# Two square sums of a hybrid decoder step in column groups, and its key pages dealt out differently

## What is computed

```python
h = x
for i in range(2):
    hn = rms_norm(h, g_pre[i])
    if i == 0: out, s = gla_mixer(hn, ...)       # q, k, v, g projections, recurrence, output projection
    else:      out = sb_mixer(hn, ...)           # q1, g1 projections, attention over K, V, output projection
    h = h + out
    h = h + sigmoid(rms_norm(h, g_ple[i]) @ w_ple_gate[i]) * (p[i] @ w_ple_up[i])
    if i == 0: k_new, v_new = split(rms_norm(h, g_kv) @ w_kv)
return rms_norm(h, g_final), states, k_new, v_new

def rms_norm(x, g):                              # over the 1024 features of a token
    return x * rsqrt(mean(x * x, axis=-1) + 1e-6) * g
```

## Time and profile before

| | |
|---|---|
| median of 3 runs | 893.49 us (893.46 to 893.99) |
| the profiled execution | 891.69 us, span of its trace 890.0 us |
| mean granted TensorE clock | 0.991 |
| busy: PE, DVE, ACT, POOL | 846.0, 553.3, 456.5, 277.9 us |
| HBM traffic | 231.6 MB, 260 GB/s |

### The profile page before, as it was taken

The page is one execution under the profiler, slowest core; times in us unless marked ns, Lnnn a source line. Parts: engine busy times, 40 slices in busy tenths (PEclk is TensorE's granted clock), DMA queues, the critical chain, the costliest instruction groups (busy, mean ns, idle before and its releaser), DMA issues.

```text
span 890.0 us, 14818 instructions
## 1 busy us (share of the span) xinstructions
PE 846.0 (95%) x5057; PEld 586.4 (66%) x5057; DVE 553.3 (62%) x678; ACT 456.5 (51%) x1529; POOL 277.9 (31%) x149
## 2 busy tenths in 40 slices
PE   5999999999999999999998999999989999999995
PEld 3666667767754444454487878778744444799995
DVE  4555475679856869989995632232267777555553
ACT  5611382236658677759772422212288766444433
POOL 3000000865776998994970000000100000021110
PEclk9999999999999999999999999999999999999997
DMA  9799868656599998988995069998898879221202
GB/s 332 273 372 399 314 228 286 215 156 216 187 311 368 377 329 306 333 330 312 344 385 189 1 234 327 357 342 305 306 331 296 320 272 362 101 95 49 95 1 96
DMA packets 109531, 232.52 MB, mean 261 GB/s; under 512 B 7473, under 2 KB 66680, under 8 KB 109456
## 3 DMA queue, kind: packets, MB, share of 16 engines
q1 hardware_dynamic: 50992, 172.16, 53.1%
q10 hardware_dynamic: 58464, 59.41, 20.0%
HBM read 220.41 MB, written 11.14 MB: 260 GB/s over the span
## 4 chain that ended last, share of the span: by engine, by line
PE 71%; DVE 8%; DMA 7%; ACT 6%; issue 4%; POOL 2%; SPq 1%; ACTq 0%; POOLq 0%; DVEq 0%
PE pp L1659 18%; PE pp L1646 15%; PE pp L1662 9%; PE pp L2080 6%; PE pp L2037 4%; DMA s<-in_state_gla_dram 3%; POOL slot L621 2%; PE pp L2064 2%; DMA slot<-in_cache_k_dram 2%; PE pp L1623 2%; PE pp L1643 2%; PE pp L2051 2%; PE pp L1674 2%; DMA slot<-in_cache_v_dram 1%; ACT slot L827 1%
## 5 line engine op out<-in xcount | busy, mean ns | idle before, releaser
L621 POOL TENSOR_TENSOR slot<-slot,qb 128x1024 f32<-128x1024 f32 x95 | 246.9, 2629 | 101.8 <-DMA slot<-in_cache_k_dram 62.9
L1307 DVE TENSOR_REDUCE zall<-slot 128x16 f32<-128x1024 f32 x99 | 119.1, 1215 | 21.7 <-POOL slot L621 20.6
L1122 DVE TENSOR_TENSOR w_lo<-w_raw,w_hi 128x1024 fp32r<-128x1024 f32 x57 | 80.0, 1405 | 68.0 <-ACT w_hi L671 67.8
L827 ACT ACTIVATE slot<-slot 128x64 f32<-128x64 f32 x464 | 111.0, 241 | 20.5 <-POOL slot L621 20.5
L671 ACT CAST w_hi<-w_raw 128x1024 fp32r<-128x1024 f32 x58 | 60.5, 1045 | 79.0 <-PE pp L1662 47.1
L827 ACT ACTIVATION_READ_ACCUMULATOR slot<-slot 128x1 f32 x464 | 87.1, 188 | 0.0
L1646 PE MATMUL pp<-xn,w_raw 128*128 128x512 f32 x192 | 84.3, 593 | 0.5 <-ACT xn L682 0.5
L1646 PE MATMUL pp<-xn,w_unsplit 128*128 128x512 f32 x192 | 83.9, 592 | 0.0
L1662 PE MATMUL pp<-xa_hi,w_hi 128*128 128x512 f32 x200 | 81.5, 407 | 1.9 <-DVE w_lo L1122 1.9
L1659 PE MATMUL pp<-xb_hi,w_hi 128*128 128x260 f32 x384 | 78.9, 287 | 1.1 <-DVE w_lo L1122 0.9
L1662 PE MATMUL pp<-xa_hi,w_lo 128*128 128x512 f32 x200 | 79.2, 396 | 0.0
(11 more groups left out here) (321 smaller groups left out, 1435.8 us busy)
## 6 DMA issues: line engine op xcount, KB each, us to landing
slot<-in_cache_k_dram SPq DMA_DIRECT2D x128, 512.0 KB, 5.9
slot<-in_cache_v_dram SPq DMA_DIRECT2D x120, 512.0 KB, 5.8
w_raw<-in_gla_w_in_dram ACTq DMA_DIRECT2D x12, 1024.0 KB, 8.7
slot<-in_gla_w_in_dram SPq DMA_DIRECT2D x24, 512.0 KB, 9.4
w_raw<-in_w_kv_dram ACTq DMA_DIRECT2D x8, 1024.0 KB, 10.9
w_raw<-in_w_ple_gate_dram ACTq DMA_DIRECT2D x6, 1024.0 KB, 5.3
s<-in_state_gla_dram SPq DMA_DIRECT2D x1, 4096.0 KB, 27.3
out_dram<-s ACTq DMA_DIRECT2D x4, 1024.0 KB, 10.1
```

What stands on the lines that cost most here:

```text
L621: nc.gpsimd.tensor_tensor(slot[s][:], slot[s][:], qb[:, (n // NPG) % 2, :], ALU.mult).then_inc(S("k_mul_pool"), 1)
L827: ins = nc.scalar.activation(part, part, ACT.Copy, accum_out=zall[:, n % NPG, b * SH + h:b * SH + h + 1])
L1122: nc.vector.tensor_tensor(lo, raw, hi.bitcast(F32), ALU.subtract).then_inc(S("w_split"), 1)
L1307: nc.vector.tensor_reduce(zall[:, n % NPG, b * SH:(b + 1) * SH], at.rearrange("p (h d) -> p h d", d=HD), AX.X, ALU.add).then_inc(S("k_used ...
```

## The change

It does two things.

*Square sums of norms 1 and 2.* The squares go into a buffer of eight tiles (`sqt`). Four of them at a time are multiplied by 32 columns of ones, each into its own quarter of the partitions of the bank (`square_parts`): one part when four tiles are there, the second part when eight are. ACT copies the accumulated quarters to SBUF, and one full sum with the matrix of ones adds them up (`square_whole`), with the mean's factor divided by 32. The second part stands behind all tiles of ple0's (or q1's) first job, the full sum behind the first two tiles of its second job.

*Pages.* Pages for each job, before and after: v 0,0,0,0,1,3,2,2 becomes 0,0,0,0,2,3,3,3; g 2,3,2,3,2,3,2,3 becomes 3 throughout; ple0 4 becomes 3; g1 4,0,... becomes 4,1,0,...; wo0 and q1 stay at 4. The pages that ACT sums are now listed: besides those of before also the first page of v jobs 5 to 7 and g jobs 0 to 2 (none before), and `sum_page` is called at the end of each v and g job's part of ACT's queue. In all, ACT sums 35 pages (29 before), POOL multiplies 103 (95), DVE multiplies 25 (33) and reduces 93 (99).

The diff, without two renamed semaphores:

```diff
--- before.py
+++ after.py
@@ -57,6 +57,7 @@
 S_BLOCKS = [(name, k) for name, n in S_STAGES for k in range(n)]
+SQ_PARTS, SQ_WHOLE = {1: (KT + 1, KT + 2), 2: (KT + 4, KT + 5)}, {0: KT, 1: KT + 3, 2: KT + 6}
 S_FIRST = {name: sum(n for _, n in S_STAGES[:i]) for i, (name, _) in enumerate(S_STAGES)}
@@ -65,10 +66,13 @@
 PAGES_AT = {}
-for _name, _c in (("v", (0, 0, 0, 0, 1, 3, 2, 2)), ("g", (2, 3, 2, 3, 2, 3, 2, 3)), ("wo0", (4,) * 8), ("ple0", (4,) * 8),
-                  ("q1", (4,) * 8), ("g1", (4, 0, 0, 0, 0, 0, 0, 0))):
+ACT_SUMS = {}
+for _name, _c, _a in (("v", (0, 0, 0, 0, 2, 3, 3, 3), (0, 0, 0, 0, 0, 1, 1, 1)),
+                      ("g", (3,) * 8, (1, 1, 1, 0, 0, 0, 0, 0)), ("wo0", (4,) * 8, (1,) * 8),
+                      ("ple0", (3,) * 8, (1,) * 8), ("q1", (4,) * 8, (2, 1) * 4), ("g1", (4, 1, 0, 0, 0, 0, 0, 0), (1,) + (0,) * 7)):
     for _u in range(PHASES[_name][1]):
         PAGES_AT[PHASES[_name][0] + _u] = _c[_u]
+        ACT_SUMS[PHASES[_name][0] + _u] = _a[_u]
 PAGES_THROUGH = {}
@@ -163,8 +167,7 @@
-    return any(len(pages_at(j)) >= 4 and n in pages_at(j)[:2 if phase_of(j) == "q1" and j % 2 == 0 else 1]
-               for j in PAGES_THROUGH)
+    return any(n in pages_at(j)[:ACT_SUMS.get(j, 0)] for j in PAGES_THROUGH)
@@ -325,6 +328,7 @@
         oP = offA + size([P, KT, T])
+        sqt = at("sqt", [P, KT, T], F32, offB + size([P, KT, T]))
         pin0 = at("pin0", [P, TB, PLE], F32, oP)
@@ -513,7 +517,7 @@
                 if s == 8 and SLOT_TURN[NSB + n] == 1:
-                    sp.wait_ge(S("sq_summed"), 3 * KT)
+                    sp.wait_ge(S("sq_summed"), SQ_WHOLE[2])
                     sp.wait_ge(S("mm"), tiles_through(PHASES["K"][0]))
@@ -688,21 +692,31 @@
                         act.wait_ge(S("sq_added"), (KT - 1) * norm + tile + 1)
-                elif n >= 2:
+                elif 2 <= n < KT:
                     act.wait_ge(S("sq_summed"), n - 1)
-                nc.scalar.activation(work[:, n % 2, 0:tokens_of((0, 2, 3, 5, 6)[n // KT])], src, ACT.Square).then_inc(S("sq"), 1)
+                elif n >= 2 * KT:
+                    act.wait_ge(S("sq_summed"), SQ_PARTS[1][1] if n < 3 * KT else SQ_PARTS[2][1])
+                sq = sqt[:, n % KT] if KT <= n < 3 * KT else work[:, n % 2]
+                nc.scalar.activation(sq[:, 0:tokens_of((0, 2, 3, 5, 6)[n // KT])], src, ACT.Square).then_inc(S("sq"), 1)
...
+                if i in SQ_PARTS:
+                    act.wait_ge(S("sq_summed"), SQ_PARTS[i][1])
+                    if i == 1:
+                        nc.scalar.copy(sqacc[:, 0:NP_TOK], bank[7]).then_inc(S("sq_part"), 1)
+                    else:
+                        nc.scalar.copy(halves(sqacc[:]), pp[3][:, :, 0:H2]).then_inc(S("sq_part"), 1)
                 if i < 3:
-                    act.wait_ge(S("sq_summed"), KT * (i + 1))
+                    act.wait_ge(S("sq_summed"), SQ_WHOLE[i])
                 else:
...
                 t = NP_TOK if i < 2 else T
+                mean = 1.0 / (SW * D) if i in SQ_PARTS else 1.0 / D
                 if i < 2:
-                    own.then(nc.scalar.activation(rstd[:, 0:t], bank[7], ACT.Ln, bias=epsc[:], scale=1.0 / D))
+                    own.then(nc.scalar.activation(rstd[:, 0:t], bank[7], ACT.Ln, bias=epsc[:], scale=mean))
                 else:
-                    own.then(nc.scalar.activation(halves(rstd[:]), pp[3][:, :, 0:H2], ACT.Ln, bias=epsc[:], scale=1.0 / D))
+                    own.then(nc.scalar.activation(halves(rstd[:]), pp[3][:, :, 0:H2], ACT.Ln, bias=epsc[:], scale=mean))
                 nc.scalar.activation(rstd[:, 0:t], rstd[:, 0:t], ACT.Exp, scale=-0.5).then_inc(S("r_root"), 1)
@@ -841,6 +855,7 @@
                 v_rows(u - 1)
+                sum_page(PHASES["v"][0] + u)
@@ -889,6 +904,7 @@
                         o_rms(h - 1)
+                sum_page(PHASES["g"][0] + u)
             act.wait_ge(S("gated"), GH - 1)
@@ -1689,18 +1705,31 @@
-            def add_squares(i, k):
-
-                n = i * KT + k
-                pe.wait_ge(S("sq"), n + 1)
-                if i and k == 0:
+            def add_squares(k):
+
+                pe.wait_ge(S("sq"), k + 1)
+                nc.tensor.matmul(bank[7], ones[:], work[:, k % 2, 0:NP_TOK], start=(k == 0),
+                                 stop=(k == KT - 1)).then_inc(S("sq_summed"), 1)
+
+            def square_parts(i, part):
+
+                pe.wait_ge(S("sq"), i * KT + (part + 1) * GH)
+                if part == 0:
                     pe.wait_ge(S("r_root"), i)
-                sq, flags = work[:, n % 2, :], dict(start=(k == 0), stop=(k == KT - 1))
-                if i < 2:
-                    nc.tensor.matmul(bank[7], ones[:], sq[:, 0:NP_TOK], **flags).then_inc(S("sq_summed"), 1)
-                    return
-                for t in range(2):
-                    last = nc.tensor.matmul(pp[3][:, t, 0:H2], ones[:], sq[:, t * H2:(t + 1) * H2], **flags)
+                for t in range(i):
+                    for g in range(GH):
+                        sq = sqt[:, part * GH + g, 0:NP_TOK] if i == 1 else sqt[:, part * GH + g, t * H2:(t + 1) * H2]
+                        out = bank[7][SW * g:SW * (g + 1), :] if i == 1 else pp[3][SW * g:SW * (g + 1), t, 0:H2]
+                        last = nc.tensor.matmul(out, ones[:, 0:SW], sq, start=(part == 0), stop=(part == 1),
+                                                skip_group_check=True)
+                last.then_inc(S("sq_summed"), 1)
+
+            def square_whole(i):
+
+                pe.wait_ge(S("sq_part"), i)
+                for t in range(i):
+                    sq = sqacc[:, 0:NP_TOK] if i == 1 else sqacc[:, t * H2:(t + 1) * H2]
+                    last = nc.tensor.matmul(bank[7] if i == 1 else pp[3][:, t, 0:H2], ones[:], sq, start=True, stop=True)
                 last.then_inc(S("sq_summed"), 1)
@@ -1760,9 +1789,9 @@
                 if k >= 2:
-                    add_squares(0, k - 2)
-            add_squares(0, KT - 2)
-            add_squares(0, KT - 1)
+                    add_squares(k - 2)
+            add_squares(KT - 2)
+            add_squares(KT - 1)
             pe.wait_ge(S("s_hs"), 1)
@@ -1964,27 +1993,33 @@
                 product(wo + u, KT)
-                add_squares(1, u - 3)
-            add_squares(1, KT - 3)
+                if u == 6:
+                    square_parts(1, 0)
             up_tile0(0)
             up_tile0(1)
-            add_squares(1, KT - 2)
             for u in range(8):
...
                     product(PHASES["ple0"][0], 2 * KT, wait_x=True, tiles=range(KT - 2))
-                    add_squares(1, KT - 1)
                     product(PHASES["ple0"][0], 2 * KT, wait_x=True, tiles=range(KT - 2, KT))
+                    square_parts(1, 1)
                 else:
-                    product(PHASES["ple0"][0] + u, 2 * KT)
+                    product(PHASES["ple0"][0] + u, 2 * KT, tiles=range(2) if u == 1 else range(KT))
+                if u == 1:
+                    square_whole(1)
+                    product(PHASES["ple0"][0] + u, 2 * KT, tiles=range(2, KT))
                 if u >= 2:
                     up_tile0(u)
-                    add_squares(2, u - 2)
+                if u == 6:
+                    square_parts(2, 0)
             for u in range(8):
...
                     product(PHASES["q1"][0], 3 * KT, wait_x=True, tiles=range(KT - 2))
-                    add_squares(2, KT - 2)
-                    add_squares(2, KT - 1)
                     product(PHASES["q1"][0], 3 * KT, wait_x=True, tiles=range(KT - 2, KT))
+                    square_parts(2, 1)
+                elif u == 1:
+                    product(PHASES["q1"][0] + u, 3 * KT, tiles=range(2))
+                    square_whole(2)
+                    product(PHASES["q1"][0] + u, 3 * KT, tiles=range(2, KT))
                 else:
```

More of the change, by code:

```diff
@@ L1364, in _ @@
             attm = attmask[:].bitcast(I32).unsqueeze(1).to_broadcast([P, TB, P])
-            dve.wait_ge(S("att_zero"), 1)
+            dve.wait_ge(S("masks"), 2)
             for u in range(8):
@@ L2104, in _ @@
                     pe.wait_ge(S("zs_out"), 4)
-                    pe.wait_ge(S("zs_pad"), 1)
+                    pe.wait_ge(S("masks"), 3)
                 if i >= 8:
```

4 lines of the change are left out of this document (2 added, 2 removed).

## The result

| | before | after |
|---|---|---|
| median | 893.48 us (4 runs, 887.79 to 893.99) | 899.64 us (4 runs, 898.57 to 904.12) |
| ratio | | 1.0092, interval 1.0061 to 1.0123 |
| profiled execution, its span | 891.69, 890.0 us | 899.57, 897.9 us |
| mean granted TensorE clock | 0.991 | 0.985 |

The change makes the kernel slower by 6.2 us in the medians and 7.9 in the two profiled executions. Foreseen were 3.3, with the same sign. The forecast's 896.8 is 2.8 us short.

A forecast was written before the change was run, and what follows sets the result against it. The tensor engine, busy in 95% of the span, was taken as the bound. Terms -6.5 + 0.6 (square sums) + 8.2 + 1.0 (pages) = +3.3 us on 891.69 gave 895.0, as a median 896.8; range 889.0 to 900.5.

The forecast's parts named there:

- The page part: v and g stages: moved pages and ScalarE page sums make the tensor engine 8.2 us late, plus 1.0 of lowered clock.
- The low half behind eight pages: Second g job: eight pages instead of six precede the vector engine's low half, so the tensor engine starts 5.9 us late.
- the page sum ahead of weight 5's high half: Second pair of g jobs: sums of 3.81 us in ScalarE's queue put the high half's end at 221.6.
- The last x tile: Gate's first job: ScalarE writes this tile only by 320.4, leaving a gap of 1.9 us, with 0.6 taken for lowered clock.
- rival D: Square sums: column groups run one after another, 4 x 0.86 us a part; part 1 loses 2 us, 905; chance 0.02.
- The second g product: Early g stage: its start was forecast near 183.0, 5.9 us late, at least 3.8.
- the slot of page 2: Before the second g job: ScalarE's 3.81 us sum holds this slot until 170.3, so page 6 loads only about 174.6.
- The gating: After the second pair of g jobs: releases the tensor engine at 225.8, 8.2 us late, with the engine idle from 220.0.
- rival B: Half of the page lateness: shorter low halves, copies released at 201.4; lateness 5.5 us, total 893; chance 0.18.
- the term of part 1: Square sums take 8.5 us off the tensor engine; 6.5 arrive by the next projection, less 0.6 for lowered clock.
- In that long stretch every microsecond of tensor work removed is a microsecond gained: Between 200 and 466 us, where the tensor engine has one gap of half a microsecond, removed work counts fully.
- the 2.69 us gap at the fourth g1 job: At 469.53, behind the vector engine: the gap stays the same and part 1's gain of 6.5 us carries through it.

The follow-up runs named there:

- e12_spread_more: `e8_spread` with wo0 ending on 3 and 2 pages, q1 taking 3 in its last four jobs, g1 3, 3, 3, 2; 889.09 us, ratio to before 0.9957.
- e2_pages: Kernel before with the change's page lists and ScalarE page sums, its own full square sums kept; 902.25 us, ratio to before 1.0090.
- e1_sums: Changed kernel with the page lists of before, so the new square sums alone; 892.87 us, ratio to before 0.9996.
- e8_spread: `e1_sums` with three pages in the last two wo0 and q1 jobs and 3, 3, 2 in g1; 888.39 us, ratio to before 0.9943.
- e11_spread_alone: Kernel before, its own square sums kept, with the page lists of `e8_spread`; 889.27 us, ratio to before 0.9945.
- e5_light_before: Kernel before with page multiplications over a quarter of the columns on GpSimd and the vector engine; 883.14 us, ratio to before 0.9884.
- e6_light_sums: `e1_sums` with page multiplications over a quarter of the columns on GpSimd and the vector engine; 876.33 us, ratio to before 0.9818.
- e9_light_dve: Changed kernel with quarter-width page multiplications and the six new ScalarE page sums in v and g moved to the vector engine; 876.31 us, ratio to before 0.9791.
- e10_v_old: Changed kernel with v's list of before (1, 3, 2, 2, no ScalarE sums there), g's new list kept; 901.32 us, ratio to before 1.0073.
- e4_early: `e1_sums` with the second part between tiles 5 and 6 of the next projection's first job, full sum right behind that job; 892.61 us, ratio 0.9987.

## Why the prediction was right or wrong

**What held.** The page part was worked out to 9.2 us of lateness at the end of g, with lowered clock; the traces show 8.8. The low half behind eight pages was one cause in that stage, and the page sum ahead of weight 5's high half the other: the queue order and the 3.8 us were right. Not named was the page sum ahead of the value copy, which made the first and longest wait, 3.52 us. The last x tile did make a gap, and it was the scalar engine's `xn` that ended it. The four 32-column products do run side by side, so rival D is out.

**What held only in its sum.** The second g product was to start near 183 and started at 180.63, 3.6 us late instead of 5.9: the slot of page 2 held nothing up, as GpSimd multiplied nine pages without a pause, from 157.26 to 179.49. The gating was to release the tensor engine at 225.8 after 5.8 us of idle; it did so at 223.32 after 3.16. That is 5.7 late instead of 8.2, and close to rival B's 5.5, by B's condition: the copies of the head came at 200.22, where the forecast had 203.2 and B 201.4. The other 3.1 us lie in the clock behind this gap: its stretch at a mean of 0.83 loses 3.4 us, where I had taken 1.0. Two errors of 2.5 and 2.1 us cancelled. The gaps behind my rows of 0.91 were single ones below 3 us; here they were 3.5 plus 1.5 us, and 1.1 plus 3.2.

There is luck in the 8.8 too. The trace of before has a lowered clock behind its wait of 1.95 us at 192.90. Of the five other traces that have the same lists up to there and full page work, all have this wait (1.94 to 1.96 us), but only that of `e12_spread_more` has the lowered clock. Counted from the samples' stage (98.28 before) to wo0's landmark, it and before took 170.4 and 170.3 us, the other four 168.0 to 168.3, the changed kernel 179.2 and `e2_pages` 177.2. So the pages cost 6.8 to 11.2 us there, by which executions are compared; the median of `e2_pages` is 8.6 above that of before.

**What failed: the term of part 1.** It stood in the sum with -6.5 + 0.6 = -5.9 us. In the traces it measured 3.3 us between the landmarks (241.60 us before, 238.29 after), in those of `e1_sums` 3.9 and of `e8_spread` against `e11_spread_alone` 4.5, and in the medians 0.8 (`e1_sums`, by its interval from 1.4 lost to 2.1 gained) and 0.9 (`e8_spread` against `e11_spread_alone`). In the changed kernel it can be followed. At q1's start, 395.33 (388.94 before), 2.4 us were won since wo0's landmark. The gap at the last x tile was 3.2 us with 1.8 of clock instead of 1.9 with 0.6: 2.5 of the 3.5 missing; three parts at 0.25 to 0.3 us more than priced: 0.8; 0.2 I can't place. Behind q1's start 0.9 came back. The gap at the fourth g1 job was 1.86 us instead of 2.69 and left no mark in the clock, which is worth 2.6; two new waits of 0.54 and 0.22 us took 0.8 of it and the fourth part 0.3, and 0.6 I can't place. The trace of `e1_sums`, that execution below all others of its kernel, won 5.5 us up to q1's start and had lost 1.7 of them again at K. The step that failed is the sentence "In that long stretch every microsecond of tensor work removed is a microsecond gained". I read it from a tensor engine without idle time. But an engine that never waits shows only that the others keep up, not with how much to spare. The rows for the answer were there: GpSimd busy 37.35 of 40 us. I used them for one tile and not for the 200 us around it. The light kernels show it: with the multiplications a quarter as wide on GpSimd and the vector engine, the same edit is worth 6.8 us. The forecast also let the 2.69 us gap at the fourth g1 job stay as it was, with the gain "carried through it", because the same page work stands ahead of it. It is that page work that doesn't come earlier by all of the time won: its last reduction began 3.0 us earlier in `e1_sums`.

**A smaller size.** In the traces of the three light kernels with the sums, the tensor engine has no gap from wo0's landmark to K. This stretch is 229.66, 229.66 and 229.68 us, against 237.00 without the sums, so the edit is worth 7.3 us on the tensor engine when nothing else holds it, not 8.5. In the light kernel with the sums a part begins at 365.43 and the next product at 366.45, so 1.02 us instead of 0.91:

```profile
363.62 1.88 PE L1690 MATMUL pp<-pT,w_up 128*128 128x512 f32 x4
365.43 1.09 PE L1723 MATMUL pp<-sqt,ones 128*32 128x260 f32 x16
366.45 7.13 PE L1662 MATMUL pp<-xn,w_unsplit 128*128 128x512 f32 x16
373.42 1.88 PE L1690 MATMUL pp<-pT,w_up 128*128 128x512 f32 x4
375.13 7.03 PE L1662 MATMUL pp<-xn,w_raw 128*128 128x512 f32 x16
382.09 1.09 PE L1723 MATMUL pp<-sqt,ones 128*32 128x260 f32 x16
```

The eight products behind it took 373.42 - 366.45 = 6.97 us where others take 6.87. And what stands ahead of a part takes 0.1 us more as well: the up product 365.43 - 363.62 = 1.81 us, where the next one, ahead of a full product, takes 375.13 - 373.42 = 1.71, and the eight products from 375.13 on 6.96. So a part costs 0.25 to 0.3 us more than its place in a stream of its own kind, some 1.1 us for four. I had given 0.4 for this. The Trainium skill (TensorEngine Tiling (Array Packing), Key Properties) says that a change of tiling mode drains the engine; by these rows the trace agrees, in that about 0.1 us is lost on either side; that it is a drain the rows can't tell. With the 1.1 us the 8.5 become 7.4.

**The rest.** From K to the end the changed kernel lost another 2.4 us in its trace. No part of the change reaches there. Its rows show where: it waited 0.80 us for a value page at 530, where before waited 0.27, and it ran 1.7 us longer behind a wait that both kernels have, because the clock fell there (before, after, and the changed kernel's stretch):

```profile
656.23 0.22 PE L2033 MATMUL pp<-maskneg,identb 128*128 128x128 bf16 x1 [2.39 <-ACT pat L1043]
```

```profile
662.60 0.26 PE L2068 MATMUL pp<-maskneg,identb 128*128 128x128 bf16 x1 [2.41 <-ACT pat L1059]
```

```profile
660.00:680.00 20.00, 17.40 (x107) 9.43 (x104) 13.77 (x24) 15.42 (x34) 0.00 (x0) 0.91 0.78 286
```

All 14 traces have this wait, of 2.39 to 2.41 us. In seven the clock then stayed at 1.00 (before, `e1_sums`, `e2_pages`, `e5_light_before`, `e6_light_sums`, `e9_light_dve`, `e11_spread_alone`), in the seven others a stretch around it has 0.91. At full page work the clock fell in six of the seven kernels with the new sums and in none of the three without; with light work in one of the three with them. Whether that is chance, one trace each can't say. It matters for the sums: between the landmarks the traces of the sums as the change places them show 3.3 to 4.5 us gained, the medians 0.8 and 0.9, and no run settles where the rest goes. The difference of the medians, 6.2 us, is nearer to the 5.5 at K than to the 7.9 at the end.

So the size of the loss comes out: pages 8.8 us (foreseen 9.2), sums 0.8 by the medians and 3.3 by the traces (foreseen 5.9).

## What to carry to other kernels

Before counting work taken off the busiest engine as time gained, read how near the others are in the same stretch: here, with two engines at 83 and 84%, only 3 to 4.5 us of seven arrived in the traces and less than one in the medians. A cheap way to find out is to make the second engine's work light in both kernels and compare them; its difference is what the edit is worth when nothing else holds it. Small work put on an idle engine costs by its place in that engine's queue: 3.8 us ahead of a copy or a weight half that the busiest engine needs were paid nearly in full here, and then once more in the clock.

## What the hardware showed that I had not expected

- **The clock's price is not one size, and a gap's length alone does not give it.** The plainest case is the wait of 2.4 us behind K: the same in 14 traces, followed by the lowered clock in seven of them, at some 1.6 us. Elsewhere, two gaps that come to 4.2 or 5.1 us within 20 us stand beside a mean of 0.83 (3.4 us lost) in the changed kernel, but two of 1.73 and 2.96 us beside 0.91 in `e2_pages`. The changed kernel's 3.21 us at the last x tile, and the 2.69 us of before, stand beside 0.91 (1.8 us). But the changed kernel's 1.86 us at the fourth g1 job, 3.12 us at the last x tile of `e10_v_old` and 3.18 us at the fourth g1 job of `e4_early` left 1.00, so cost only themselves. The stretch of `e10_v_old`:

```profile
320.00:340.00 20.00, 16.88 (x46) 6.80 (x45) 14.96 (x14) 14.50 (x75) 20.00 (x8) 1.00 0.92 339
```

  From these traces a single gap of 1.9 to 3.2 us can be priced only as a range: nothing to 1.8 us.
- **At the lowered clock a group of four column tiles takes twice its time like everything else:** 1.94 us as shown by its row in the changed kernel, against 1.07 in `e6_light_sums` (at 295.23).
- **A narrow sum with an accumulator is slow on ScalarE.** Each of the 16 instructions over 64 elements takes 0.24 us in sequence, 3.8 us a page, where the vector engine reduces the whole page in 1.22 us. Ahead of something urgent in the same queue, that is what it costs.
